# The HGRN sigmoids of a four-layer float32 kernel: from exp, add, reciprocal to tanh and one fused instruction

## What is computed

```python
def hgrn2_mixer(xn, w_q, w_f, w_i, w_g, g_norm, w_o, lb):
    q = jax.nn.silu(xn @ w_q)                               # z * sigmoid(z)
    forget = lb + (1.0 - lb) * jax.nn.sigmoid(xn @ w_f)
    k = 1.0 - forget
    v = xn @ w_i
    # linear recurrence over time: state = forget * state + k v^T, o = q . state
    o = rmsnorm(o, g_norm)
    gate = jax.nn.silu(xn @ w_g)
    return (o * gate) @ w_o
```

## Time and profile before

| | |
|---|---|
| median of three runs | 1634.16 us |
| the profiled execution | 1640.71 us, its span 1638.9 us |
| PE busy | 1439.8 us, 88% |
| DVE busy | 1117.1 us, 68% |
| ACT busy | 599.0 us, 37% |
| mean DMA rate | 160 GB/s |
| share of the chain that ended last | PE 68%, DVE 23%, ACT 3% |

### The profile page before, as it was taken

One profiled execution on the slowest core, in us unless ns is written; L12 is line 12 of the kernel. 1 busy time (PEld: TensorE's weight loads), 2 busy tenths in 40 slices (PEclk: granted clock), 3 DMA queues, 4 the chain that ended last, 5 costly groups with the idle time before them and its releaser, 6 DMA issues.

```text
span 1638.9 us, 22629 instructions
## 1 busy us (share of the span) xinstructions
PE 1439.8 (88%) x8726; PEld 1268.0 (77%) x8726; DVE 1117.1 (68%) x1619; ACT 599.0 (37%) x788; POOL 2.9 (0%) x5
## 2 busy tenths in 40 slices
PE   1788989999898798999959785799998798989997
PEld 1755769999786676999949785699997676879996
DVE  6879778776887448655579998555556745475555
ACT  1432333343334223343344221433335454343332
POOL 0000000000000000000000000000000000000000
PEclk9985589999898758999979998799999999989999
DMA  9543536767376202655515421145553321445540
GB/s 363 213 167 111 172 116 254 272 246 267 116 294 245 90 26 99 229 189 189 181 51 204 152 78 52 52 180 193 188 183 129 119 87 52 139 153 183 182 176 26
DMA packets 44671, 262.91 MB, mean 160 GB/s; under 512 B 5045, under 2 KB 6709, under 8 KB 18870
## 3 DMA queue, kind: packets, MB, share of 16 engines
q1 hardware_dynamic: 31792, 217.01, 36.6%
q10 hardware_dynamic: 12810, 44.95, 7.7%
HBM read 260.89 MB, written 1.05 MB: 160 GB/s over the span
## 4 chain that ended last, share of the span: by engine, by line
PE 68%; DVE 23%; ACT 3%; issue 3%; DMA 2%; ACTq 0%; SPq 0%; DVEq 0%
PE bank L517 20%; PE bank L518 19%; PE bank L519 19%; DVE w_lo L1288 3%; PE bank L650 3%; DVE A L1302 3%; DVE A L1447 2%; DMA A<-ada_w 2%; ACT w_hi L912 1%; PE bank L668 1%; PE bank L623 1%; DVE A L1722 1%; DVE hT_lo L1277 1%; PE bank L679 1%; PE bank L678 1%
## 5 line engine op out<-in xcount | busy, mean ns | idle before, releaser
L1288 DVE TENSOR_TENSOR w_lo<-raw,w_hi 128x2048 fp32r<-128x2048 f32 x193 | 440.0, 2287 | 163.4 <-ACT w_hi L912 160.9
L912 ACT ACTIVATE w_hi<-raw 128x2048 fp32r<-128x2048 f32 x193 | 369.4, 1914 | 257.2 <-PE bank L519 215.0
L517 PE MATMUL bank<-hT_hi,w_hi 128*128 128x256 f32 x1432 | 417.3, 291 | 11.0 <-DVE hT_lo L1617 9.5
L518 PE MATMUL bank<-hT_lo,w_hi 128*128 128x256 f32 x1432 | 412.3, 288 | 0.0
L519 PE MATMUL bank<-hT_hi,w_lo 128*128 128x256 f32 x1432 | 412.1, 288 | 0.0
L517 PEld LDWEIGHTS bank<-hT_hi,w_hi 128*128 128x128 f32 x1432 | 282.6, 197 | 17.3 <-issue 9.5
L518 PEld LDWEIGHTS bank<-hT_lo,w_hi 128*128 128x128 f32 x1432 | 282.6, 197 | 3.8 <-issue 1.5
L519 PEld LDWEIGHTS bank<-hT_hi,w_lo 128*128 128x128 f32 x1432 | 282.0, 197 | 0.0
L517 PE MATMUL bank<-w_hi,R 128*128 128x512 f32 (+1 forms) x560 | 218.7, 390 | 1.3 <-DVE R L1277 1.3
L518 PE MATMUL bank<-w_lo,R 128*128 128x512 f32 (+1 forms) x560 | 217.7, 389 | 0.0
L519 PE MATMUL bank<-w_hi,R 128*128 128x512 f32 (+1 forms) x560 | 217.0, 388 | 0.0
(11 more groups left out here) (192 smaller groups left out, 1544.9 us busy)
## 6 DMA issues: line engine op xcount, KB each, us to landing
raw<-stream SPq DMA_DIRECT2D x193, 1024.0 KB, 4.8
A<-ada_w ACTq DMA_DIRECT2D x73, 512.0 KB, 5.3
A<-ada_w SPq DMA_DIRECT2D x9, 1024.0 KB, 8.5
A<-ln_g ACTq DMA_DIRECT2D x4, 512.0 KB, 3.7
A<-ln_b ACTq DMA_DIRECT2D x4, 512.0 KB, 5.4
A<-ada_w SPq DMA_DIRECT2D x1, 1536.0 KB
A<-x_t SPq DMA_DIRECT2D x1, 1024.0 KB, 12.5
X<-ada_w SPq DMA_DIRECT2D x1, 1024.0 KB
```

The source lines that it names most:

```text
L517: pe.matmul(o, lh, rh, start=start, stop=False, skip_group_check=True)
L518: pe.matmul(o, lh, rl, start=False, stop=False, skip_group_check=True)
L912: act.activation(w_hi[:, s, :], raw[:, s, :], ACT.Copy).then_inc(hi_done, 1)
L1288: v.tensor_tensor(w_lo[:, s, :], raw[:, s, :], w_hi[:, s, :], ALU.subtract).then_inc(lo_done, 1)
```

## The change

All three sigmoids use sigmoid(z) = (1 + tanh(z/2)) / 2. ACT writes tanh(z/2) instead of exp(-z), and its copy of z is scaled by 0.5. DVE's addition and reciprocal go; for silu and gate the multiplication becomes one `scalar_tensor_tensor`, (tanh + 1) * (z/2). For forget the factor and the offset in `lb_c` are changed to (1 - lb)/2 and (1 + lb)/2, which takes one small instruction more at the start.

```diff
@@ ACT, a sigmoid fill
                         if reader == "silu":
-                            act.activation(dst, bank[:, :], ACT.Copy)
+                            act.activation(dst, bank[:, :], ACT.Copy, scale=0.5)
                         elif reader == "gate":
-                            act.activation(dst, two(bank[:, :]), ACT.Copy)
-                        act.activation(e, bank[:, :], ACT.Exp, scale=-1.0).then_inc(e_done, 1)
+                            act.activation(dst, two(bank[:, :]), ACT.Copy, scale=0.5)
+                        act.activation(e, bank[:, :], ACT.Tanh, scale=0.5).then_inc(e_done, 1)
@@ DVE, a sigmoid fill
                         v.wait_ge(e_done, n["e"])
-                        link(v.tensor_scalar(e, e, 1.0, None, ALU.add))
-                        link(v.reciprocal(e, e))
                         if reader == "silu":
-                            v.tensor_tensor(dst, dst, e, ALU.mult).then_inc(silu_done, 1)
+                            v.scalar_tensor_tensor(out=dst, in0=e, scalar=1.0, in1=dst, op0=ALU.add,
+                                                   op1=ALU.mult).then_inc(silu_done, 1)
                         elif reader == "gate":
-                            link(v.tensor_tensor(dst, dst, two(e), ALU.mult))
+                            link(v.scalar_tensor_tensor(out=dst, in0=two(e), scalar=1.0, in1=dst, op0=ALU.add,
+                                                        op1=ALU.mult))
@@ DVE, hg_start
-                    link(v.tensor_scalar(lb_c[:, 1, :], lb_c[:, 0, :], -1.0, 1.0, ALU.mult, ALU.add))
+                    link(v.tensor_scalar(lb_c[:, 1, :], lb_c[:, 0, :], -0.5, 0.5, ALU.mult, ALU.add))
+                    link(v.tensor_scalar(lb_c[:, 0, :], lb_c[:, 0, :], 0.5, 0.5, ALU.mult, ALU.add))
```

## The result

The changed kernel takes 1614.83 us, the median of four runs, against 1636.36 us of the kernel before beside it. The ratio is 0.9849 with a 95% interval of 0.9825 to 0.9873, which is 21 to 29 us. The two medians themselves are 21.5 us apart, at the small end of that interval. A second comparison, with five runs of the changed kernel, gave 0.984 (0.9826 to 0.9854), 26 us. Two executions of the experiments' kernels (5793.9 us for the change in the gate units alone, 2460.3 us for one more instruction in them), with a mean granted clock of 0.23 and 0.75 instead of 0.91, stand in no ratio. The profiled execution of the change has a span of 1618.0 us, 20.9 less than the one before.

The account below looks back on a forecast made before the run. PE bounds the first part, then a wait before level 0, then DVE bounds the levels. 10.3 us from the wait and its clock plus 14.1 from the levels give 24.4: 1634.2 to 1609.8 us, range 1604 to 1618.

Parts of the forecast that it names:

- The sum: Whole kernel: 24.4 us gained, 10.3 from the wait and its clock, 14.1 from the level part; median 1609.8 us; chance 0.75.
- The first part: Silu and forget units: DVE carries no debt, level 0 starts 8.5 us earlier and gains 1.8 us of clock, 10.3 together.
- The limit passes to PE: Levels: PE sets the pace at 9.26 us against DVE's 9.07; level 5 starts on DVE 24.5 us earlier.
- The end of the levels: Levels 5 to 7 and one low part on DVE: 17.4 us to the output products, PE's groups ready in time.
- could gain 1.8: The 16 output products at 1008.76 take 3.55 us at half clock and could gain 1.8 us.
- The operations: Fused instruction 692 ns, tanh 0.59 us, small `lb_c` instruction 0 because hidden, no table load.
- the one that the prediction named: DVE's idle 0.81 us for ACT before the first silu unit, said to hide the small `lb_c` instruction.
- Only the stall goes: Levels: DVE's freed time turns into another wait, only 10.3 us gained, 1623.9 us; chance 0.04.
- Tables change at every tanh: ACT: each tanh brings two table loads, 2.57 us; only the last gate unit's 1.3 us shows, 1611.1 us; chance 0.06.
- A fused instruction of double length: DVE: fused instruction runs in two passes, 0.6 us in the last gate unit, 0.4 a level, 1612 us; chance 0.02.
- Half clock in the level part: PE in the levels: two to four half-clock stretches cost 3.6 to 7.2 us, 1613 to 1617 us; chance 0.1.
- Slower: PE, busy without a pause, gets half the clock throughout 918 to 968 us, costing 50 us, 1660 us; chance 0.03.

Follow-up runs that it names:

- e4: The changed kernel with two more DVE multiplications in each of the eight silu and forget units; ratio 0.9848 to the kernel before.
- the last experiment: The changed kernel with the stage's last low part on DVE moved from behind level 5 to behind level 7; 1612.87 us, ratio 0.9821 to the kernel before.

## Why the prediction was right

**The sum.** Forecast were 24.4 us; the two comparisons give 24.7 (1.51% of 1636.4) and 26.3 us (1.6% of 1642.1), with intervals that hold 24.4. The forecast time of 1609.8 is 5 us under the measured 1614.8, because the median of the kernel before was itself 2.2 us higher in that comparison, and because the two medians are 21.5 us apart and not 24.4; this 2.9 us lies within the scatter of single runs (1608.55 to 1619.82).

**The first part.** "Level 0 starts 8.5 us earlier, and 1.8 us come from its clock": measured 8.4 and 1.8. The halves of the change show it alone with 10.25 us for the forecast 10.3.

**The limit passes to PE.** Forecast was level 5 on DVE 24.5 us earlier than before; measured from the value fill it is 24.2. The period of a level and its fill is 9.33 us (921.55 to 930.88), not 9.26: the first matmul behind a level takes 0.20 us to the next one's start (925.04 to 925.24), the others of the fill 0.12. The kernel before has the same 9.33 us from level 1 to level 2 on PE (937.51 to 946.84). That also corrects a reading: PE there waited for DVE not from level 2 on but from the second group of level 3 on (0.71 us), which changes no term of the sum. Of the 15.4 us removed in the gate units 13.9 are gained up to level 5, and 1.5 became waits, forecast 1.3. That the margin of PE is small was right as well: one more instruction of 0.72 us in each gate unit, 2.9 us in all, put level 5 off by 1.5.

**The end of the levels was mis-sized.** The prediction took 17.4 us from level 5 to the output products "with PE's groups ready in time". It is 18.5. The ranges allowed for a stretch at half clock in this part, but not where it would count: before the change it lay on PE's level 6, which ran beside DVE's work on level 5 and the low part and was done in time; now it falls on level 7, where DVE has nothing else to do and waits 1.04 us. In the profiled execution the output products gave it back, with 2.05 us at full clock instead of 3.55, which the range had as "could gain 1.8". That the two errors cancel is luck: in e4, whose PE work is that of the changed kernel, the 16 output products took 3.58 us to the next group's start, in the changed kernel 1.89.

**The operations.** The fused instruction takes 692 ns, as taken. Tanh takes 592 ns, as exp did. The small instruction on `lb_c` takes 0.17 us, and DVE's next wait, for ACT's high part, shrinks from 1.54 to 1.34 us; it is this wait that covers it, ahead of the one that the prediction named. No table load was added, also in the two kernels in which exp and tanh follow each other. The Trainium skill, "ScalarE: Activation LUTs", Table sets, puts tanh and exp in one set; by that rule there was no load to come, and the trace agrees: three loads before, three after.

**The rivals.** Only the stall goes: out, by the gate units' 13.05 us. Tables change at every tanh: out, by the three loads. A fused instruction of double length: out, by its 692 ns. Half clock in the level part in two to four stretches: there was one, on level 7, and it cost 1.04 us. Slower, by half clock throughout: out; PE is busy from 876.6 to 971.0 us without a pause, and the granted clock of that stretch is 1.00.

## What to carry over

Two engines that are both near 100% busy in a stretch need not share the path: find the one whose work the other is waiting for at the stretch's end, and the time freed on the other is worth only that wait and what the wait costs in clock (here 8.4 and 1.8 us for 30.8 removed). Where an operation is removed from the bound, work out the next engine's period for the same loop step before multiplying, since here 15.4 us removed were worth 13 to 14. And time freed where nothing counts can still be used: look for a piece of the late part that may be done in an idle place, as the low part was.

## What the runs showed of the hardware

DVE's reciprocal of 512 float32 a partition takes 3.35 us, nearly five times the 0.69 us of an instruction with two inputs of that size and nearly eight times the 0.43 us of an addition of a constant; ACT's tanh costs no more than its copy (0.59 and 0.60 us).

In this stage the granted clock went to half only near pauses of PE, and a shorter pause can be worth more than itself. With a stall of 8.28 us the level behind it ran in 5.57 us, without in 3.74. What pause it takes wasn't settled. In the last levels pauses of 1.59, 0.47 and 2.65 us were followed by a group at half clock, pauses of 1.59, 0.47, 0.46 and 0.45 us were not; and behind a pause of 2.94 us the output products ran in 3.55 us in the kernel before and in 2.05 us in the last experiment. The half-clock stretch lay on level 6, on level 7 or on the output products in kernels that differ by 1 us.

The span ahead of the stage, in which the kernels are the same, is 862.9 to 869.6 us in ten profiles. These 6.7 us are more than a quarter of the effect measured here. Measured between two instructions of the stage, A repeats to 0.1 us in the two profiles of the changed kernel. Which wait ahead of it makes this scatter wasn't looked into.
